# One decoder layer on one core: the third and fourth modulation sums spread one slab per weight slab over four projection groups, with an accumulator of their own and their column sums behind the sixth group

## The reference

```python
c_act = jax.nn.silu(c)
mod = c_act @ w_mod[l] + b_mod[l]                       # (2048) @ (2048 x 12288)
shift1, scale1, gate1, shift2, scale2, gate2 = ...split(mod, 6)
h = rms_norm(x, g_pre_mix[l]) * (1.0 + scale1) + shift1
proj = h @ w_in[l]
q, k, v, q_idx, k_idx, w_idx, pool_in, lru_in, lru_gate = split_columns(proj)
attn = dsa_attention(q, k, v, q_idx, k_idx, w_idx, positions, rel_bias)
pool = pool_mixer(pool_in, ...)
lru = rglru_mixer(lru_in, lru_gate, ...)                # conv, two gates, scan, GeLU
x = x + gate1 * rms_norm(concat(norms) @ w_out[l], g_post_mix[l])
h = rms_norm(x, g_pre_mlp[l]) * (1.0 + scale2) + shift2
x = x + gate2 * rms_norm(square(relu(h @ w_mlp_up[l])) @ w_mlp_down[l], g_post_mlp[l])
```

## Time and profile before

| | us |
|---|---|
| median of 3 runs | 2305.6 (2298.7 to 2308.4) |
| the profiled execution | 2302.4 |
| its span | 2300.6 |
| PE busy | 2209.4, 96% of the span |
| DVE busy | 1842.4, 80% |
| ACT busy | 985.3, 43% |
| POOL busy | 398.9, 17% |
| mean clock granted to TensorE | 0.983 of full |

### The profile page before, as it was taken

The page is one execution under the profiler, slowest core; times in us unless marked ns, Lnnn a source line. Parts: engine busy times, 40 slices in busy tenths (PEclk is TensorE's granted clock), DMA queues, the critical chain, the costliest instruction groups (busy, mean ns, idle before and its releaser), DMA issues.

```text
span 2300.6 us, 39123 instructions
## 1 busy us (share of the span) xinstructions
PE 2209.4 (96%) x15364; PEld 1985.7 (86%) x15364; DVE 1842.4 (80%) x2096; ACT 985.3 (43%) x1201; POOL 398.9 (17%) x278
## 2 busy tenths in 40 slices
PE   6899999999999999989999999999899999999996
PEld 2457787888777788889999999999899999999996
DVE  6749984997447674798999999999777888878788
ACT  4334325222347421655555555555433333333442
POOL 6540034444347000000000000000000011212120
PEclk8999999999999999999999999999999999999998
DMA  9877665335533397326656555555935636528434
GB/s 359 324 300 265 247 241 120 92 92 194 193 122 96 129 354 240 128 74 207 206 205 205 191 192 194 191 192 204 399 135 205 272 111 244 201 106 318 158 111 165
DMA packets 180656, 459.02 MB, mean 200 GB/s; under 512 B 17712, under 2 KB 76720, under 8 KB 168368
## 3 DMA queue, kind: packets, MB, share of 16 engines
q1 hardware_dynamic: 117104, 389.60, 47.4%
q10 hardware_dynamic: 63424, 67.64, 8.6%
HBM read 381.42 MB, written 75.51 MB: 199 GB/s over the span
## 4 chain that ended last, share of the span: by engine, by line
PE 51%; DVE 3%; DMA 2%; issue 1%; ACT 1%; DVEq 0%; ACTq 0%
PE psum L1041 17%; PE psum L1042 17%; PE psum L1043 17%; DMA u2f<-f_lo 1%; DMA T_parts<-u2f 1%; DVE w_lo L2464 0%; DVE B_raw L2730 0%; DVE T_parts L2714 0%; DVE f_lo L2509 0%; DVE x_odd L2610 0%; ACT w_hi L1776 0%; DVE y_half L2576 0%; DVE y_half L2598 0%; DVE y_half L2588 0%; DVE raw L2610 0%
## 5 line engine op out<-in xcount | busy, mean ns | idle before, releaser
L1019 POOL TENSOR_TENSOR y_half<-y_half,part 128x512 f32<-128x512 f32 x44 | 87.2, 1993 | 1395.4 <-DVE y_half L2621 1395.4
L1041 PE MATMUL psum<-T_parts,w_hi 128*128 128x256 f32 x1024 | 290.0, 283 | 10.8 <-DVE u_t L2747 5.1
L1041 PE MATMUL psum<-w_hi,T_parts 128*128 128x256 f32 x1024 | 290.6, 284 | 2.6 <-DMA T_parts<-u2f 2.6
L1042 PE MATMUL psum<-w_lo,T_parts 128*128 128x256 f32 x1024 | 290.0, 283 | 0.0
L1043 PE MATMUL psum<-T_parts,w_lo 128*128 128x256 f32 x1024 | 289.4, 283 | 0.0
L1042 PE MATMUL psum<-T_parts,w_hi 128*128 128x256 f32 x1024 | 289.3, 283 | 0.0
L1043 PE MATMUL psum<-w_hi,T_parts 128*128 128x256 f32 x1024 | 287.7, 281 | 0.0
L1488 ACT ACTIVATE w_hi<-raw 128x1024 fp32r<-128x1024 f32 (+1 forms) x128 | 129.4, 1016 | 335.4 <-PE psum L1043 275.6
L970 POOL TENSOR_TENSOR w_lo<-raw,w_hi 128x1024 fp32r<-128x1024 f32 (+1 forms) x80 | 190.5, 2388 | 371.3 <-ACT w_hi L1488 371.3
L1041 PE MATMUL psum<-h_hi,w_hi 128*128 128x512 f32 (+1 forms) x592 | 239.8, 405 | 8.8 <-issue 4.4
L1042 PE MATMUL psum<-h_lo,w_hi 128*128 128x512 f32 (+1 forms) x592 | 237.6, 401 | 0.0
(11 more groups left out here) (362 smaller groups left out, 5649.2 us busy)
## 6 DMA issues: line engine op xcount, KB each, us to landing
raw<-in_w_in SPq DMA_DIRECT2D x88, 512.0 KB, 5.5
mod_ring<-in_w_mod_first SPq DMA_DIRECT2D x32, 1024.0 KB, 9.6
mod_slab<-in_w_mod SPq DMA_DIRECT2D x32, 1024.0 KB, 5.3
raw<-in_w_up_units SPq DMA_DIRECT2D x64, 512.0 KB, 5.4
unit_odd<-in_w_up_units SPq DMA_DIRECT2D x64, 512.0 KB, 5.9
raw<-in_w_down_units SPq DMA_DIRECT2D x64, 512.0 KB, 5.5
unit_odd<-in_w_down_units SPq DMA_DIRECT2D x64, 512.0 KB, 5.8
T_parts<-u2f SPq DMA_DIRECT2D x32, 1024.0 KB, 14.7
```

The costliest lines, as they stand in the source:

```text
L1019: nc.gpsimd.tensor_tensor(y, y, part[:], ALU.add).then_inc(y_pool, 1)
L1041: nc.tensor.matmul(o, a_hi, b_hi, start=first, stop=False)
L1042: nc.tensor.matmul(o, a_hi, b_lo, start=False, stop=False)
```

## The change

The 32 sums of mod2 and mod3 now stand one beside each slab from 16 to 47, that is over g2, g3, g4 and g5. mod2 uses `acc_a` as before; mod3 gets an accumulator of its own, `acc_c` at 152 KB, where before it shared `acc_b` at 12 KB with mod4 (and with `lru_o`, which is why DVE waited for mod3's stage ahead of `lru_o`; that wait is gone). PE's column sums of mod3 stand behind g6 instead of behind the two gate products, `STAGES` is changed to match, and so the psum banks of g5 and g6 change places. DVE's `mod_out(3)` moves from behind the first gate step to the place after 24 of the 64 top-k rounds.

```diff
-MOD_MORE = SG
+MOD_MORE = KD
+MOD3_AT = 68
...
-    if 2 * SG <= s < 4 * SG:
-        i = s - 2 * SG
-        first = MOD_EARLY + 3 * (i // 2) + 2 * (i % 2)
-        return [first] if i % 2 else [first, first + 1]
-    if MOD_AGAIN <= s < MOD_AGAIN + MOD_MORE:
-        return [MOD_EARLY + 3 * SG + s - MOD_AGAIN]
+    if 2 * SG <= s < 2 * SG + 2 * KD:
+        return [MOD_EARLY + s - 2 * SG]
     return []
...
-    + [("g3", "A"), ("mod2", "D"), ("g4", "A"), ("rgate", "A"), ("igate", "A"), ("mod3", "D"), ("g5", "A"), ("g6", "A"),
+    + [("g3", "A"), ("mod2", "D"), ("g4", "A"), ("rgate", "A"), ("igate", "A"), ("g5", "A"), ("g6", "A"), ("mod3", "D"),
...
+        acc_c = at(152, "acc_c", [P, D], F32)
...
+        def acc_of(j):
+
+            return {2: acc_a, 3: acc_c, 4: acc_b}[j]
...
-            mod_sum(3)
             group(G_POOL, STAGE["g5"], features_out, h)
             group(G_K, STAGE["g6"], features_out, h)
+            mod_sum(3)
...
             dve.sem_inc(branch_dve, 1)
-            mod_out(3)
...
-            wait_stage(dve, "mod3")
             ch.link(V.scalar_tensor_tensor(lru_o[:], r_t[:], 0.5, gate_in[:], ALU.mult, ALU.mult))
...
+            s = beside_to(s, MOD3_AT)
+            mod_out(3)
             s = beside_to(s, TOPK_AT + TT * ROUNDS // 2)
```

More of the change, by code:

```diff
@@ L1080, in mod_sum @@
                 pe.wait_ge(mod_step, KD * (j + 1) - MOD_EARLY)
-                acc = acc_a if j == 2 else acc_b
+                acc = acc_of(j)
                 for k in range(KD):
```

## The result

| | us |
|---|---|
| changed kernel, median of 19 runs | 2311.0 (2304.1 to 2318.8) |
| kernel before, median of 19 runs, the three above among them | 2300.3 (2292.5 to 2308.4) |
| ratio, changed to before | 1.0048, 95% interval 1.0037 to 1.0060 |
| the profiled execution of the changed kernel | 2306.9, span 2305.1 |

By the ratio the change costs 11.0 us, with an interval of 8.5 to 13.8 (the two medians differ by 10.7). The forecast time of 2310.8 agrees with the measured 2311.0 by luck, because two misses cancel: the runs of the kernel before stood at 2300.3 this time, not at 2305.6, and the cost was 11.0 us, not 5.2. It is the cost that has to be explained.

A forecast was written before the change was run, and what follows sets the result against it. PE, busy for 96% of the span, was taken as the bound. Being 9.7 us later by g7, less 4.5 from g2, gave 5.2 us slower: median 2305.6 becomes 2310.8, range 2300 to 2317.

The forecast's parts named there:

- Fewer sums in g2: Ahead of g3: PE's gap falls from 4.4 to 1.8 us; gain taken as 4.5 us, ends 2.6 and 4.6.
- mod_sum(2): Ahead of g4: PE waits 0.9 us for the sum beside slab 31; ends 0 and 2.
- r_t later: Three more sums ahead of `r_t`, paced by their loads, start it 8.3 us later; bound 5.8 to 11.7.
- Rival (c): Ahead of `r_t`: slab loads share DMA engines with modulation slabs; landings of 8.6 give 8.6 us slower; chance 0.07.
- Slabs 43 and 45: In g5: PE waits 4.8 us ahead of slab 43 and 2.1 us ahead of slab 45.
- rival (b): Slab 45 in g5: its low part waits out a DVE sum, 1.9 us more, net 7.1 us slower; chance 0.14.
- The clock in g5 and g6: From slab 45 at 389.3, g5 ends at 406.2 and g6 at 451.2; g7 starts 5.1 us later.
- The sum: At g7's start: 9.7 us later than before; less 4.5 from g2, 5.2 us slower.
- the gain of g2: The 4.5 us gained ahead of g3, subtracted whole at the end from the 9.7 us.
- Costs put at nothing: Remaining sums up to slab 51, slab loads on SP's queue, and `mod_out(3)` ahead of g8: cost 0 each.
- (a): Ahead of `r_t` and slab 45: the delay is hidden, g2's gain stays, 3.7 us faster (2301.9); chance 0.17.
- (d): In g2: DVE is not relieved because the sums wait for loads; chance 0.02 together with anything else.

The follow-up runs named there:

- the kernel with the four narrow sums: Kernel before with four of g2's twelve modulation sums made over 256 of the 2048 columns, loads unchanged; ratio 0.9983.
- the kernel with column sums and delay: Kernel before with mod3's column sums behind g6, its own accumulator and late `mod_out(3)`, plus five unused DVE products ahead of `r_t`; ratio 1.0030.
- the one with the late store: Changed kernel with SP's store of the first gate vector moved from beside slab 44 to beside slab 56; ratio 1.0051.

## Why the prediction was right and where it was wrong

I take the steps in the order of the prediction, each behind the place where it starts. "First" and "second" are the two executions of the changed kernel.

**Fewer sums in g2.** Right. The gap came to 1.79 us (forecast 1.8). The end of g3 comes 3.0 us sooner in the first and 4.6 us in the second, the forecast's ends being 2.6 and 4.6 (by the one trace of before, with the caution above). Which end one gets is the clock: the same 1.79 us gap was followed by a granted clock of 0.88 from 226 to 240 us in the first, and of 1.00 in the second and in the kernel with the four narrow sums.

**mod_sum(2).** Right: a wait of 0.77 us, forecast 0.9.

**r_t later.** The mechanism was right, the size was not, and this is the first term that failed. From the end of g3 to `r_t` it was 59.7 us before. It is 362.57 - 291.87 = 70.7 in the first (292.64 less the wait of 0.77 is 291.87) and 70.2 in the second. That is 11.0 and 10.5 us later, not 8.3; it lies inside the stated bound of 5.8 to 11.7. Two pieces make the miss. The fifth sum, from which the three follow, was to start 1.1 us sooner behind g3 than before; it started 1.2 us later in the first and at the same time in the second. And the three steps behind it took 13.75 and 14.45 us, not 13.1. The 13.1 was three times the mean of the last two steps of before, with the last load of that row issued at 341.55 and the DMA engines nearly idle from 352 us on. In the changed kernel four more modulation slabs follow by 359 us, each with a weight slab but the last. From 325 to 365 us the landings are these, and from 335 to 360 the stream fills 0.84 to 0.99 of the DMA engines' time:

```profile
DMA to landing us min/median/max: 5.0/7.0/8.3
```

In the same row of before the three landings had a median of 6.3. Rival (c) named this contention and gave it 0.07; its place and its delay of 11.7 came near to what was measured, though the median landing was 7.0 and not 8.6. By the prediction's own formula a landing of 7.0 gives 9.3 us, so the formula was short too, because it took the steps up to the fifth sum as unchanged. That both pieces come from the full DMA engines is read from these shares and landings; no run took the weight slabs out of the row, so it is not shown by an experiment.

**Slabs 43 and 45.** Both gaps came, where they were forecast and ended by POOL's low part. From `r_t` to the product of slab 43 it is 11.5 us (forecast 11.6). From `r_t` to that of slab 45 it is 27.8, forecast 26.9. In the kernel with column sums and delay it is 26.3. The difference of 1.5 us is the low part of slab 45 itself, by the starts of POOL and PE:

```profile
383.32 4.82 DVE L2064 SCALAR_TENSOR_TENSOR acc_c<-mod_slab,c_act,acc_c 128x2048 f32<-128x2048 f32 x2 [0.24 <-DVE r_t L2296]
```

```profile
386.42 10.95 POOL L972 TENSOR_TENSOR w_lo<-raw,w_hi 128x1024 fp32r<-128x1024 f32 x4 [10.09 <-ACT w_hi L1490]
```

```profile
385.43 13.88 POOL L976 TENSOR_TENSOR w_lo<-raw,w_hi 128x1024 fp32r<-128x1024 f32 x5 [10.08 <-ACT w_hi L1494]
...
387.88 0.50 PE L1047 MATMUL psum<-h_hi,w_hi 128*128 128x512 f32 x1 [0.78 <-POOL w_lo L976]
```

The first two are of the changed kernel, where a sum is at work on DVE until 388.14 and PE has its slab at 390.39, 3.97 us after POOL began (3.98 in the second). The last is the kernel with column sums and delay, which has no sum there: 2.45 us from POOL's start to the product. That is rival (b), at 1.5 us (it had said 1.9 beyond 2.9; against my 2.9 it is 0.9 to 1.1). The Trainium skill, "SBUF — State Buffer", section "Who interferes with whom", says that the two engines hold the shared port one at a time. The traces fit that: POOL loses about what was left of the second sum when it began, 388.14 - 386.42 = 1.7 us.

**The clock in g5 and g6.** From slab 45's product to `mod_sum(3)` the forecast was 61.9 us. It was 63.5 in the first and 61.95 in the second. In the first the granted clock was 0.66 from 390 to 395 us, behind the gap. `mod_sum(3)` and g7 together then took 48.8 and 50.3 us, forecast 50.1. So these two executions each lose about 1.5 us at one of the two places; the one with the late store lost it at both (63.5, and 51.9 for the second).

**The sum.** Forecast 5.2 us. First: 1.5 for the gain at g2 not had, 2.7 for `r_t`, 0.9 for the low part, 1.6 and -1.4 for the clock: 5.2 + 5.3 = 10.5, as measured. Second: -0.1, 2.2, 0.9, 0.1 and 0.1 in the same places: 5.2 + 3.2 = 8.4, and 8.5 was measured. The runs gave 11.0 with an interval from 8.5, so the profile accounts for it within its error.

**Whether the gain of g2 was kept.** It was subtracted from the whole, and that step holds: the branch moves with PE. With four narrow sums in the kernel before it was kept in full. In the changed kernel it is still there when the row of eight sums begins, 3.7 us sooner than before behind the first product of g2 in the first execution (328.44 - 168.37 against 331.69 - 167.92), 6.2 in the second (327.80 - 170.22). Then the row takes 34.1 and 34.6 us up to `r_t`; the prediction's numbers make it 31.8 (from 330.6 to 362.4). The row does not take back what was won ahead of it: in the second execution it begins 2.5 us sooner than in the first, and `r_t` comes 2.0 us sooner (192.2 against 194.2). So the 2.3 to 2.8 us are the row's own length, mis-sized, and they hide a gain that is there. No run has the row of eight sums with the full gap at g2, which would show it outright.

**Costs put at nothing.** Right: no gap at slab 51, none ahead of g7 or g8, and the store late or early makes no difference in the changed kernel. They were near to an edge, though. With three sums more behind the scan, slab 51 waited 6.66 us.

**Rivals.** (a) is refuted: the delay was not hidden. (b) came in part, 0.9 to 1.1 us of its 1.9. (d) is refuted: the gap fell to 1.79. The range of 2300 to 2317 held the median, but the forecast's own range of 2.7 to 8.6 us slower did not hold the cost of 11.0. The prediction took 0.5% as the least that could be told from no change; the 19 runs of each kernel told 0.37 to 0.60%.

## What to carry to other kernels

Sums that are fed by loads cost what their bytes cost once the loads come in a row: count all that the queue sends with each of them, divide by the bandwidth that the windows show, and compare this with the engine time before calling a slot free. Take the pace from a stretch that is as long and as full as the new one will be, not from the end of a row. Making the work itself smaller without its loads shows which of the two paces it. Moving work off PE's way to a place behind a wait on another engine is not neutral: it lengthens that wait, and is paid again where it now stands.

## What the hardware showed that I had not expected

A store of 8 KB in 4-byte elements took 15.3 us to land in the changed kernel, and behind it the DMA engines were busy for 0.50 and 0.85 of the time while they moved 10 and 40 GB/s (windows 380 to 384 and 384 to 388 us). With slabs due behind it on the same queue, moving it away took the ratio from 1.0078 to 1.0050, two intervals that just overlap; where no slab was due, it changed nothing.

```profile
gate_s<-mod SPq DMA_DIRECT2D x1, 8.0 KB, 15.3
```

The granted clock from 226 to 240 us, around the same 1.79 us gap of PE, was 1.00 in seven traces and 0.88 in two, both of those of kernels with the changed kernel's list up to there, as are four of the seven. What decides between them, no run here shows.
